# Banded attention in units of two query blocks, admitted with every second projection

## The reference, cut to what matters

```python
def banded_attention(q, k, v, max_dist, sinks=None):
    ...
    s = jnp.einsum('bnjqhgd,bnjkhd->bnjhgqk', qb, kb) * scale
    ...
    dist = qpos - kpos
    mask = (dist >= 0) & (dist <= max_dist) & (kpos >= 0)
    s = jnp.where(mask[:, None, None, :, :], s, jnp.float32(NEG))
    m = jnp.max(s, axis=-1, keepdims=True)
    ...
        m = jnp.maximum(m, sk)
        p = jnp.exp(s - m)
        denom = jnp.sum(p, axis=-1, keepdims=True) + jnp.exp(sk - m)
    ...
    o = jnp.einsum('bnjhgqk,bnjkhd->bnjqhgd', p / denom, vb)

def first_block(...):
    h = rmsnorm(x, ln1_g[l])
    qa, ka, va, qb, kb, vb, ga, gb = jnp.split(h @ w_in[l], offsets, axis=-1)
    ...
    oa = dilated_attention(qa, ka, va)
    ob, _ = banded_attention(qb, kb, vb, SWA_WINDOW - 1, sinks[l])
    mix = jax.nn.sigmoid(ga) * (oa @ w_branch_a[l]) + jax.nn.sigmoid(gb) * (ob @ w_branch_b[l])
    x = x + mix @ w_out[l]
    h2 = rmsnorm(x, ln2_g[l])
    x = x + jnp.square(jax.nn.relu(h2 @ w_up[l])) @ w_down[l]
```

## Time and profile before

| | |
|---|---|
| median of 3 runs | 2397.43 us (2397.34 to 2400.26) |
| the profiled execution's own time | 2398.88 us |
| its span in the trace | 2397.0 us |
| PE busy | 2371.4 us (99%) |
| DVE busy | 1211.2 us (51%) |
| ACT busy | 965.3 us (40%) |
| POOL busy | 1321.9 us (55%) |
| granted clock of PE | 0.999 |

### The profile page before, as it was taken

The page is one execution under the profiler, slowest core; times in us unless marked ns, Lnnn a source line. Parts: engine busy times, 40 slices in busy tenths (PEclk is TensorE's granted clock), DMA queues, the critical chain, the costliest instruction groups (busy, mean ns, idle before and its releaser), DMA issues.

```text
span 2397.0 us, 29725 instructions
## 1 busy us (share of the span) xinstructions
PE 2371.4 (99%) x11108; PEld 1922.4 (80%) x11108; DVE 1211.2 (51%) x1968; ACT 965.3 (40%) x1513; POOL 1321.9 (55%) x1589
## 2 busy tenths in 40 slices
PE   8999999999999999999999999999999999999999
PEld 8777778888888888777788888888887777788887
DVE  5998775423224533378624843333325785266330
ACT  4554453322223223466524432332336764344321
POOL 5763246656556655466345765555554562466554
PEclk9999999999999999999999999999999999999999
DMA  4321123333333333222122333333332221323333
GB/s 159 109 72 56 49 76 98 91 99 97 96 99 108 96 97 104 79 63 79 54 81 87 97 97 97 97 97 97 97 95 71 71 77 51 93 88 97 97 97 97
DMA packets 59758, 213.40 MB, mean 89 GB/s; under 512 B 6624, under 2 KB 6752, under 8 KB 59488
## 3 DMA queue, kind: packets, MB, share of 16 engines
q1 hardware_dynamic: 59472, 211.38, 29.4%
q10 hardware_dynamic: 144, 0.14, 0.0%
HBM read 209.39 MB, written 2.10 MB: 88 GB/s over the span
## 4 chain that ended last, share of the span: by engine, by line
PE 90%; DVE 6%; issue 2%; ACT 1%; POOL 1%; DMA 0%; SPq 0%; DVEq 0%; ACTq 0%
PE banks L723 89%; DVE t L1206 1%; DVE t L1214 1%; DVE t L1216 1%; POOL t L2009 1%; DVE t L1207 0%; DVE t L1222 0%; PE banks L843 0%; ACT t L1696 0%; DVE t L1200 0%; DVE t L1504 0%; PE banks L997 0%; DVE t L1225 0%; DMA t<-in_w 0%; PE banks L877 0%
## 5 line engine op out<-in xcount | busy, mean ns | idle before, releaser
L723 PE MATMUL banks<-t,t 128*128 128x512 f32 (+5 forms) x10788 | 2343.2, 386 | 17.2 <-ACT t L1716 6.0
L723 PEld LDWEIGHTS banks<-t,t 128*128 128x128 f32 (+2 forms) x10788 | 1887.4, 188 | 445.9 <-issue 54.9
L2009 POOL TENSOR_TENSOR t<-t,t 128x256 fp32r<-128x256 f32 x1544 | 1263.6, 849 | 1034.8 <-ACT t L1696 1026.5
L1696 ACT ACTIVATE t<-t 128x1024 fp32r<-128x1024 f32 x385 | 408.0, 1060 | 1065.5 <-issue 597.4
L1200 DVE TENSOR_TENSOR t<-banks,t 128x512 f32<-128x512 f32 x121 | 83.0, 686 | 163.4 <-PE banks L723 162.8
L1381 DVE TENSOR_TENSOR t<-banks,t 128x512 f32<-128x512 f32 x44 | 30.4, 691 | 184.1 <-PE banks L723 184.0
L1349 DVE SCALAR_TENSOR_TENSOR t<-banks,t 128x512 f32<-128x512 f32 x32 | 22.1, 692 | 155.4 <-PE banks L723 155.4
L1083 DVE SCALAR_TENSOR_TENSOR t<-t,t,t 128x512 fp32r<-128x512 f32 x64 | 52.7, 827 | 57.3 <-ACT t L1716 57.3
L1326 DVE TENSOR_TENSOR t<-t,t 128x512 fp32r<-128x512 f32 x68 | 70.5, 1037 | 2.3
L1355 DVE TENSOR_TENSOR t<-banks,t 128x512 f32<-128x512 f32 x24 | 16.6, 692 | 106.0 <-PE banks L723 106.0
L1716 ACT ACTIVATE t<-t,t 128x512 fp32r<-128x512 f32 x64 | 45.6, 715 | 55.9 <-DVE t L1349 49.1
(11 more groups left out here) (186 smaller groups left out, 1307.8 us busy)
## 6 DMA issues: line engine op xcount, KB each, us to landing
t<-in_w SPq DMA_DIRECT2D x386, 512.0 KB, 3.5
t<-in_xT SPq DMA_DIRECT2D x8, 256.0 KB, 5.8
out<-t SPq DMA_DIRECT2D x8, 256.0 KB, 4.4
t<-in_dmask SPq DMA_DIRECT2D x1, 1536.0 KB, 7.5
t<-in_vbias SPq DMA_DIRECT2D x2, 384.0 KB, 4.1
t<-in_c SPq DMA_DIRECT2D x1, 576.0 KB, 8.7
t<-in_w SPq DMA_DIRECT2D x2, 256.0 KB, 3.8
t<-in_pos SPq DMA_DIRECT2D x2, 256.0 KB, 4.2
```

The source lines that it names most:

```text
L723: return pe.matmul(o, l, r, start=start, stop=stop, skip_group_check=True)
L1696: a.activation(whl[u % 2][:, 0:1024], wraw[u % 3][:, :], ACT.Copy).then_inc(*w_high.next(u))
L2009: p.tensor_tensor(hl[:, 1024:2048][:, c], wraw[u % 3][:, c], as_f32(hl[:, c]), ALU.subtract).then_inc(*w_low.next((u, q)))
```

## The change

A banded item becomes a unit (i, u) of two query blocks, 2u and 2u + 1, of head pair i; there are 8 for 16. Its scores fill up to 512 columns of each of the slot's two banks (unit 0 leaves out the block that query block 0 doesn't see). The softmax steps run over both blocks at once, with four row statistics instead of two; maximum with the sink and negation are one instruction per head, and the sink's exponential takes the sink as its bias, which drops L1295. Six or eight transposes go into both banks, ScalarE copies each, and the values come by key block: `SWA_BLOCKS` lists the key blocks that are turned, and `SWA_VALUES` gives for each key block the columns of the turned scores, their width and where in the output they add. The copy out takes 256 columns. The scratch area of a slot is one tile of 1024 columns (`SWS`), and the statistics get their own columns (`SWM`). The mask tile is filled by two transfers of 256 columns, both from the mask of the later blocks. Items are admitted behind each qa projection only.

```diff
+SWA_BLOCKS = ((1, 2, 3), (0, 1, 2, 3))
+SWA_VALUES = (((0, 0, 256, 0), (1, 256, 128, 128)), ((2, 128, 256, 0), (1, 0, 128, 0), (3, 384, 128, 128)))
...
+        SWS = [reg(88 + 6 * s, 1024)[:, :] for s in range(3)]
+        SWM = [[small_t[:, 32 + 16 * s + 4 * k:36 + 16 * s + 4 * k] for k in range(3)] for s in range(3)]
...
+            def swa_scores(i, u):
+                bk = pair(swa_at[i, u][0])
...
+                free(*bk)
+                for n, b in enumerate((2 * u, 2 * u + 1)):
+                    k0, o = 128 * max(b - 1, 0), 256 * n + (128 if b == 0 else 0)
+                    for hf in range(2):
+                        rows = slice(64 * hf, 64 * hf + 64)
+                        ins = mm(B[bk[hf]][:, o:256 * n + 256], QB[i][rows, 128 * b:128 * b + 128],
+                                 KBt[rows, k0:128 * b + 128])
...
+            def swa_turn(i, u):
...
                 for hf in range(2):
+                    for n, k in enumerate(SWA_BLOCKS[u]):
+                        ins = pe.transpose(B[bk[hf]][:, 128 * n:128 * n + 128],
+                                           SWS[slot][:, 512 * hf + 128 * k:512 * hf + 128 * k + 128], C["ident"])
...
+                for n, (k, at_, wide_, to) in enumerate(SWA_VALUES[u]):
                     for hf in range(2):
+                        ins = mm(B[ba][64 * hf:64 * hf + 64, to:to + wide_], VB[:, k, 64 * hf:64 * hf + 64],
+                                 SWS[slot][:, 512 * hf + at_:512 * hf + at_ + wide_], n == 0, n == len(SWA_VALUES[u]) - 1)
...
+            def swa_soft(i, u):
...
                 for hf in range(2):
+                    o, q = sx[:, 512 * hf:512 * hf + 512], B[pair(slot)[hf]]
+                    if u:
+                        v.scalar_tensor_tensor(out=o, in0=q, scalar=0.125, in1=swm_t[:, :], op0=M_,
+                                               op1=A_).then_inc(*v_attn.next())
+                    else:
+                        v.scalar_tensor_tensor(out=o[:, 128:512], in0=q[:, 128:512], scalar=0.125, in1=swm_t[:, 128:512],
+                                               op0=M_, op1=A_).then_inc(*v_attn.next())
...
+                if u:
+                    v.tensor_reduce(top_, sx.rearrange("p (g k) -> p g k", g=4), AX, MX).then_inc(*v_attn.next())
+                else:
+                    s2, t2 = (x.rearrange("p (h k) -> p h k", h=2) for x in (sx, top_))
+                    v.tensor_reduce(t2[:, :, 0], s2[:, :, 128:256], AX, MX).then_inc(*v_attn.next())
+                    v.tensor_reduce(t2[:, :, 1], s2[:, :, 256:512], AX, MX).then_inc(*v_attn.next())
...
+                    v.tensor_scalar(top_[:, 2 * hf:2 * hf + 2], top_[:, 2 * hf:2 * hf + 2], sk[:, hf:hf + 1], -1.0, MX,
+                                    M_).then_inc(*v_attn.next(("swa_max", i, u)))
...
+                v.tensor_tensor(sum_, sum_, sink_, A_).then_inc(*v_attn.next())
...
+                v.reciprocal(sum_, sum_).then_inc(*v_attn.next())
...
+                for g in range(4):
+                    c = slice(256 * g + (128 if u == 0 and g % 2 == 0 else 0), 256 * g + 256)
+                    v.tensor_scalar(sx[:, c], sx[:, c], sum_[:, g:g + 1], None, M_).then_inc(
+                        *v_attn.next(("swa_p", i, u)))
...
+                for g in range(4):
+                    c = slice(256 * g + (128 if u == 0 and g % 2 == 0 else 0), 256 * g + 256)
+                    a.activation(sx[:, c], sx[:, c], ACT.Exp, bias=top_[:, g:g + 1],
+                                 accum_out=sum_[:, g:g + 1]).then_inc(*a_attn.next(("swa_exp", i, u)))
...
+                for hf in range(2):
+                    a.activation(SWS[slot][:, 512 * hf:512 * hf + n], B[pair(slot)[hf]][:, 0:n], ACT.Copy).then_inc(
+                        *a_attn.next(("swa_pt", i, u)))
...
-                sp.dma_start(swm_t[:, :], smask).then_inc(*in_swm.next("swm"))
+                for n in range(2):
+                    sp.dma_start(swm_t[:, 256 * n:256 * n + 256], smask[:, 256:512]).then_inc(*in_swm.next("swm"))
...
-        banded = [swa_item(i, b) for b in range(4) for i in range(4)]
+        banded = [swa_item(i, u) for u in range(2) for i in range(4)]
...
-                sch.waiting += banded[:AFTER]
-                del banded[:AFTER]
+                if n == "qa":
+                    sch.waiting += banded[:AFTER]
+                    del banded[:AFTER]
```

More of the change, by code:

```diff
@@ L872, in swa_turn @@
-            def swa_turn(i, b):
-                slot = swa_at[i, b][0]
-                bb = pair(slot)[1]
-                need.wait_ge(*v_attn.at(("swa_p", i, b)))
-                for k in range(4):
-                    ins = pe.transpose(B[bb][:, 128 * k:128 * k + 128], reg_S[slot][0][:, 128 * k:128 * k + 128], C["ident"])
-                ins.then_inc(*t_attn.next(("swa_turn", i, b)))
-                bank[bb] = [(a_attn, ("swa_pt", i, b))]
-            def swa_values(i, b):
-                slot = swa_at[i, b][0]
+                free(*bk)
@@ new lines, in swa_scores @@
+                for n, b in enumerate((2 * u, 2 * u + 1)):
[4 more added lines that the diff above has]
+                                 KBt[rows, k0:128 * b + 128])
+                ins.then_inc(*t_attn.next(("swa_scores", i, u)))
+            def swa_turn(i, u):
+                slot = swa_at[i, u][0]
+                bk = pair(slot)
+                need.wait_ge(*v_attn.at(("swa_p", i, u)))
+                for hf in range(2):
+                    for n, k in enumerate(SWA_BLOCKS[u]):
+                        ins = pe.transpose(B[bk[hf]][:, 128 * n:128 * n + 128],
+                                           SWS[slot][:, 512 * hf + 128 * k:512 * hf + 128 * k + 128], C["ident"])
+                ins.then_inc(*t_attn.next(("swa_turn", i, u)))
+                bank[bk[1]] = [(a_attn, ("swa_pt", i, u))]
@@ L883, in swa_values @@
+            def swa_values(i, u):
+                slot = swa_at[i, u][0]
                 ba = pair(slot)[0]
-                k0 = max(b - 1, 0)
-                need.wait_ge(*a_attn.at(("swa_pt", i, b)))
+                need.wait_ge(*a_attn.at(("swa_pt", i, u)))
                 need.wait_ge(*v_evac.at(("vn", 3)))
-                for k in range(2):
+                for n, (k, at_, wide_, to) in enumerate(SWA_VALUES[u]):
                     for hf in range(2):
-                        ins = mm(B[ba][64 * hf:64 * hf + 64, 0:128], VB[:, k0 + k, 64 * hf:64 * hf + 64],
-                                 reg_S[slot][1][:, 256 * hf + 128 * k:256 * hf + 128 * k + 128], k == 0, k == 1)
@@ L1274, in dil_pt @@
                         *v_attn.next(("dil_pt1", t, r)))
-            def swa_soft(i, b):
-                slot, after = swa_at[i, b]
-                sx, c0 = reg_S[slot][0], 8 * slot
-                mk = swm_t[:, 0:256] if b == 0 else swm_t[:, 256:512]
+            def swa_soft(i, u):
+                slot, after = swa_at[i, u]
+                sx, (top_, sum_, sink_) = SWS[slot], SWM[slot]
                 sk = cols_t[:, CAT["sink"] + 2 * i:CAT["sink"] + 2 * i + 2]
-                need.wait_ge(*t_attn.at(("swa_scores", i, b)))
+                need.wait_ge(*t_attn.at(("swa_scores", i, u)))
                 need.wait_ge(*in_swm.at("swm"))
@@ L1284, in swa_soft @@
                 for hf in range(2):
-                    v.scalar_tensor_tensor(out=sx[:, 256 * hf:256 * hf + 256], in0=B[pair(slot)[hf]][:, 0:256],
-                                           scalar=0.125, in1=mk, op0=M_, op1=A_).then_inc(*v_attn.next())
-                need.wait_ge(*v_attn.last())
-                v.tensor_reduce(m2[:, c0:c0 + 2], sx[:, 0:512].rearrange("p (h k) -> p h k", h=2), AX,
-                                MX).then_inc(*v_attn.next())
-                need.wait_ge(*v_attn.last())
@@ new lines, in swa_norm @@
+            def swa_norm(i, u):
+                slot = swa_at[i, u][0]
+                sx, (top_, sum_, sink_) = SWS[slot], SWM[slot]
+                need.wait_ge(*a_attn.at(("swa_exp", i, u)))
+                v.tensor_tensor(sum_, sum_, sink_, A_).then_inc(*v_attn.next())
+                need.wait_ge(*v_attn.last())
+                v.reciprocal(sum_, sum_).then_inc(*v_attn.next())
+                need.wait_ge(*v_attn.last())
+                for g in range(4):
+                    c = slice(256 * g + (128 if u == 0 and g % 2 == 0 else 0), 256 * g + 256)
+                    v.tensor_scalar(sx[:, c], sx[:, c], sum_[:, g:g + 1], None, M_).then_inc(
+                        *v_attn.next(("swa_p", i, u)))
@@ L1316, in halves1, with swa_out @@
+            def swa_out(i, u):
+                need.wait_ge(*t_attn.at(("swa_values", i, u)))
+                v.tensor_copy(OB[i][:, 256 * u:256 * u + 256],
+                              B[pair(swa_at[i, u][0])[0]][:, 0:256]).then_inc(*v_attn.next(("swa_out", i, u)))
             def halves1():
```

54 lines of the change are left out of this document (13 added, 41 removed).

## The result

The changed kernel took 2403.84 us (median of 11 runs, 2402.07 to 2406.62), the one before 2399.41 us in the 11 runs beside it. One of those 11 took 3559.9 us in a slow state and is left out of the ratio, which is 1.0021, with an interval of 1.0012 to 1.0031: slower by 2.9 to 7.4 us. The forecast of 2387 and its range, 2383 to 2396, both missed, and the sign with them. The profiled execution took 2403.24 us.

The account below looks back on a forecast made before the run. TensorE, nine tenths of the path, was taken as the bound, with VectorE also at its limit in the first stretch. From 2398.88 us profiled, -6.6 - 3.5 - 0.5 = -10.6 us gave 2387 by the median; range 2383 to 2396.

Parts of the forecast that it names:

- TensorE's part: TensorE's own work in the banded attention: fewer columns and fewer small steps, -6.6 us, 3.5 of it before 206 us.
- columns: Fewer matmul columns on TensorE in units of blocks 0 and 1: 0.65 us each, -2.6 us for four.
- entries: Entering and leaving small TensorE steps: 24 go, at 0.17 us each, 4.0 us.
- The first rival: Only TensorE's columns are saved, small steps' entry costs being hidden: -2.6 us there, 2391 us in all; chance 0.18.
- VectorE's part: VectorE among the projections: 17.8 us of work where it had 27.2, ending 3.5 us of TensorE's idle time.
- ScalarE and GpSimd: ScalarE's load stays and its exponentials come in pieces twice as long, 2.0 us for 1.0, hidden by other work.
- the second rival: ScalarE's longer exponentials delay the projections' weights; 9.6 us come back, leaving -1.0, 2396 us, no change; chance 0.13.
- Masks: Two mask transfers of 128 KB for one of 256 KB: nothing, or 0.4 us if the cover failed.
- tail: End of the banded work: a longer last chain against an earlier start, bounds -1.2 and +3.5, taken as -0.5 us.
- The third rival: The last two units run one behind the other after the last covering gate: 2401.7 or 2404 us; chance 0.11.
- the signs named ahead: VectorE's busy time about 9 us lower, TensorE's idle time under 2, merge some 10 us earlier, 2071 us behind it.
- the warnings: Signs against: projections waiting for L2009, over 3 us bare before the last values, TensorE repeatedly over 1 us before VectorE's products.

Follow-up runs that it names:

- price of 2.1: Changed kernel, no instruction changed; the planner that orders TensorE's steps counts 2.1 us more for a unit's products: 2389.18 us.
- joined: Changed kernel with a unit's four VectorE products made into one or two with a broadcast factor; the planner's order moved too: 2388.7 us.
- joined, same order: Changed kernel with a unit's four products made into one or two, the planner told the old price so TensorE's order stays: 2393.39 us.
- filled waits: Changed kernel with three dummy fp32 matmuls before the transposes of three units, where TensorE had waited: 2399.55 us.
- admission in pairs: Kernel before, single items kept but admitted two at a time behind each qa projection: 2407.6 us.
- products cut: Kernel before with each item's two products of 256 columns cut into four of 128: 2412.99 us.
- price +1.2: Kernel before, no instruction changed; the planner counts 1.2 us more for an item's products: 2413.16 us.
- joined, price +1.0: Changed kernel with a unit's products made into one or two, and the planner counting 1.0 us more for them: 2393.24 us.
- admission undone: Changed kernel with units admitted behind every projection, qa and ka, instead of behind each qa alone: 2398.6 us.
- products on ScalarE: Changed kernel with a unit's four products moved from VectorE to ScalarE as scaled copies: 2395.27 us.
- admission undone, price +2.1: Changed kernel with units admitted behind every projection and the planner counting 2.1 us more for a unit's products: 2399.62 us.
- price +1.4: Changed kernel, no instruction changed; the planner counts 1.4 us more for a unit's products: 2393.97 us.

## Why the prediction was wrong

**TensorE's part, -6.6: right in kind, its size not settled.** TensorE's groups by shape of the kernel with the price of 2.1, from 92 to 206 us, three units of the first kind:

```profile
L729 PE MATMUL banks<-t,t 64*128 64x128 f32 x36 | 5.4, 412 | 0.0
...
L886 PE MATMUL banks<-t,t 128*128 128x128 f32 x18 | 2.4, 272 | 0.0
L729 PE MATMUL banks<-t,t 128*64 128x256 f32 x12 | 2.0, 404 | 0.0
L729 PE MATMUL banks<-t,t 64*128 64x256 f32 x12 | 1.8, 377 | 0.0
...
L729 PE MATMUL banks<-t,t 128*64 128x128 f32 x12 | 1.2, 272 | 0.0
```

Twelve of the 36 in the first row are scores of units (1.8 us as a share). Together 9.2, or 3.07 a unit, where two items took 3.96: 0.9 less, where the forecast had 0.65 of columns and 0.5 of entries. That leaves 0.24 for three entries, 0.08 each instead of 0.17, and with the columns at their 2.6 some 4.5 us for eight units. The two kernels with the least idle time agree: their rests, 2386.6 and 2383.8, are 3.5 and 6.3 under the kernel before. The first rival, by the rule that the Trainium skill gives (TensorE: Matmul & The Clock Gate, Back-to-back issue gap), had 2.6; these sizes lie between it and the forecast. Counted up to the merge, the same two kernels are 4.7 and 6.3 under the one before, and the changed kernel 7.0, close to the 6.6 of the forecast. Why the orders with more idle time show less work, down to 8 us under the kernel before in the middle of the rests, stays open.

**VectorE's part: the work was right, the step from work to idle time failed.** The three units' instructions were forecast at 17.8 us. VectorE's groups of the changed kernel from 92 to 206 us:

```profile
L1322 DVE TENSOR_SCALAR t<-t,t 128x256 f32<-128x256 f32 x6 | 5.0, 838 | 0.0
L1322 DVE TENSOR_SCALAR t<-t,t 128x128 f32<-128x128 f32 x6 | 3.6, 601 | 0.1
L1298 DVE SCALAR_TENSOR_TENSOR t<-banks,t 128x384 f32<-128x384 f32 x6 | 3.0, 543 | 0.0
...
L1306 DVE TENSOR_REDUCE t<-t 128x2 f32<-128x512 f32 x3 | 2.0, 676 | 0.0
...
L1309 DVE TENSOR_SCALAR t<-t,t 128x2 f32<-128x2 f32 x6 | 1.1, 225 | 0.1
```

With L1305 and L1327 at 1.3 each, L1316 at 1.0 and L1318 at 0.5 they come to 18.8, 8.4 less than the 27.2 of before for a forecast of 9.4, and VectorE's busy time fell by 12.4. The sentence that failed is the one behind it: "I take -3.5, nearer to the far end because the relief is almost twice the idle time", with bounds of 0 and -5.1. The idle time rose by 5.8. Idle time of TensorE in this stage isn't VectorE's load that spills over. It is single arrivals at single places. A unit doubles what one arrival waits for: four products at the port in a row, forecast at 1.1 + 4 x 0.22 = 2.0 us, took 8.6/3 = 2.9 on the mean and 3.2 where it mattered. The bound of 0 excluded a loss without naming a reason, though the prediction had itself noted that the planner's prices know no stretching. The orders with 1.9 and 2.1 us of idle time show that -5 was there to be had, in other places.

**The clock: a term of 6.7 us that the sum did not have.** The earlier trace rows show 1.00 in all stretches, and TensorE's longest wait from 60 to 350 us was 1.5 us there; nothing in the trace of before priced a longer wait.

**ScalarE and GpSimd "nothing".** The changed kernel has 1.5 us of waits for L2029 in two places; the mechanism of the second rival is there at a sixth of its price. At the changed kernel's places it is worth 3.2 us once the products are joined.

**Masks, tail.** Of waits for the mask and for the last unit's values nothing shows above: the last unit's products run from 310.6 to 313.1 us, its copy out is done by 318, and gate matmuls cover the rest of its way. TensorE waited 0.51 us for it where it waited 1.24 for the last item before; the forecast had 0.5 less for the tail. The third rival did not happen. Its figure of 2404 is what was measured, but that is luck: it came by another mechanism. Of the signs named ahead, the fall of VectorE's busy time came, larger than said, and two failed: idle time under 2 us, and a merge some 10 us earlier, which begins 5.5 us later. Two of the warnings came true: a wait for the low halves in the projections, and transposes that TensorE reaches before VectorE has their products, several times over 1 us.

**In sum**, in spans: +5.8 of idle time, +6.7 of clock, -8.2 of rest, together +4.3; the forecast had -3.5, 0 and -7.1 (-6.6 and the tail's -0.5).

## What to carry to other kernels

Where an engine's order is fixed beforehand, merging steps saves work, but it makes each arrival later and longer; go through the places one by one (what is due there, what runs beside it, how early the waiting engine comes) and don't turn an average relief into less waiting. Give a change of order a range of its own: here the same instructions in another order spread over 15 us, more than the joined products were worth at fixed places (10.4). When a series of small VectorE instructions meets GpSimd, join them into one before touching the order, and judge a change to such a kernel over several orders, not one.

## What the runs showed of the hardware

The granted clock of TensorE drops from 2.4 to 1.2 GHz behind waits, most often of 2 us and more, but not behind each of these. The traces from 60 to 350 us:

| kernel | TensorE's waits (us) behind or in which the clock dropped | longest wait with no drop right behind it |
|---|---|---|
| before; price +2.1; joined | none | 1.5; 1.3; 1.0 |
| changed | 2.5; 3.2; 2.0; 2.1 | 1.3 |
| joined, same order | none | 2.0 |
| filled waits | 2.0 | 1.3 |
| admission in pairs | 3.0; 1.8 and 1.3 close together | 1.2 |
| products cut | 3.4; 1.0 and 2.4 close together | 1.3 |
| price +1.2 | twice 1.6, close together; 3.7 | 1.8 |
| joined, price +1.0 | 2.4; 1.2 | 0.9 |
| admission undone | 3.0 and 6.1 close together | 0.4 |
| products on ScalarE | 4.1 | 0.8 |
| admission undone, price +2.1 | 2.6 (7.1 and 1.6 came while it was down) | 0.4 |
| price +1.4 | 1.7 | 2.4 |

In the three kernels whose waits were all 1.5 us or less there was no drop. In the two kernels with the same order a wait of 2.0 us had a drop behind it in one and not in the other, and with the price of 1.4 the clock stood at 1.00 from 190.4 to 195.5 us, behind a wait of 2.4. So the length of a wait alone doesn't tell whether the clock drops; what else decides is not shown. A drop gave away 1.7 us in the changed kernel, so the wait of 2.5 us cost 4.2 in all. That filling three such waits with useless matmuls makes the kernel 4.3 us faster is the same fact from the other side.

A product of VectorE over 256 columns takes 0.35 us alone and 0.81 to 0.84 beside one of GpSimd's pieces of about 0.9 us. The two joined instructions of a unit of blocks 0 and 1, over 256 and 512 columns, take 1.03 us in the first unit and 1.85 and 1.84 in the two places where the four products took 3.21 and 3.20. Four products that meet no piece take 1.14 us, over 256 columns each, so little is saved in the work itself: what joining saves is turns at the ports.
